# Differential attention in an fp32 hybrid block: where the memory's query linears stand in its pipeline, and where lambda is formed

## The chip, the cores and the metric

The kernel runs on one core of a Trainium2 chip. The metric is the device time of one execution in microseconds, and the median of several runs is compared.

## The reference, cut to what matters

Two blocks run one after the other; the change touches the second, a stack of two layers (`l` = 0, 1) over 512 tokens with 1024 features. Each layer forms many projections of the same input, among them the queries, keys and values of a differential attention and the queries of an attention over 256 memory vectors:

```python
lam = exp(sum(lf[0] * lf[1])) - exp(sum(lf[2] * lf[3])) + lam_init      # one number a layer
s = einsum('bqhcd,bkhcd->bhcqk', qi, k)        # 4 heads, two score maps c = 0, 1, 64 features each
p = softmax(s, axis=-1)
a = p[:, :, 0] - lam * p[:, :, 1]              # the two maps mixed
o = einsum('bhqk,bhkv->bqhv', a, v)
...
mx_q = x @ w_in[..., the last 512 columns]     # the memory's queries: the "query linears"
mx_o = memory_attention(mx_q, mem_k, mem_v)    # softmax over 256 memory vectors, 4 heads
```

## The kernel before, in words

Every engine has its own instruction list, written out by hand; an engine runs its list strictly in order and waits on semaphores. The order of the lists is therefore the schedule.

**Weights.** A linear in fp32 is done as three matmuls on split operands. Weights arrive in a ring of six slots (SyncE issues the loads). ScalarE rounds a slot's weights to the high part (`cast_to`, L402, tile WH), GpSimd subtracts to get the low part (`rest_to`, L411, tile WL), and TensorE uses both. WH and WL hold three pieces. `cast_to(act, n)` makes all casts up to piece n that are not made yet, where it stands in ScalarE's list.

**Token linears** (`tok_pe`, `tok_a`, `tok_v`, `tok_g`). Three groups of four pieces give the queries, keys and values. ScalarE empties their banks (L2329). VectorE rotates queries and keys (helper, L1765 to L1772), TensorE turns them per head (L2321), VectorE copies the turned queries (L2351) and ScalarE the turned keys (L2334). Lambda: a product and a sum on VectorE (L2358, L2360), Exp on ScalarE (L2337), two small operations on VectorE (L2362, L2364).

**The differential attention** (`diff`) runs over 16 items (4 heads by 4 blocks of 128 queries) as a pipeline of five stages over t = 0 to 19. At step t TensorE does, in this order, the values product of item t-4 (L2393), the turn of the mixed probabilities of item t-3 (L2386) and the scores of item t (L2379). ScalarE does the output copy of item t-4 (L2437), the copy of the turned probabilities of item t-3 (L2432) and the two Exps of item t-1 (L2425). VectorE does the two maxima of item t-1 (L2402, then L2404) and the mixing of item t-2 (L2407 to L2413).

**Beside it**, after the stages of every fourth step (`if t % 4 == 0`), one piece of other work is put in: on TensorE one of the memory's query linears (24 matmuls, L459 to L462), on ScalarE `cast_to` of the piece two further on and then the copy that empties that linear's bank (L2495). In layer 0 the first such place holds the memory's values instead (TensorE L2466, ScalarE L2478), and the four query linears follow; layer 1 begins with a query linear. Then comes `memory`, the attention over the memory, whose first scores are L2196; on VectorE the normalisation of the differential attention (L2537, L2539) stands ahead of its first maximum (L2202).

Banks are taken in turn from eight (`bank.take`), and a bank is taken again only after the copy that empties it.

Of the kernel before, what the change touches and what calls it, by code (L numbers as in the profile page):

```python
# [9 lines left out]
ALU = mybir.AluOpType  # L10
ACT = mybir.ActivationFunctionType
AX = mybir.AxisListType.X
# [32 lines left out]
ROWS = {"mla_q_norm": 0, "mla_k_norm": 96, "da_norm_g_2": 192, "hg_norm_g_2": 448, "da_lambda_2": 704}  # L45
# [231 lines left out]
def program(nc, dr, out):  # L277
    ctx = ExitStack()
    with ctx:
# [2042 lines left out]
                    m.then_inc(*da.pe.up("turn", l, h, x))  # L2322

        def tok_a(act, l):
            for g in L_tok[l].groups:
                cast_to(act, g.last + 2)
                for t in range(4):
                    act.wait_ge(*split.pe.at("used", g.last))
                    act.copy((qt, kt_, vt)[g.key][:, t, :], ps(L_tok[l].name, g.key, t)[:, :]).then_inc(  # L2329
                        *bank.emptied((L_tok[l].name, g.key, t), da.a, "tok", l, g.key, t))  # L2330
            cast_to(act, g.last + 3)
            for h in range(4):
                act.wait_ge(*da.pe.at("turn", l, h, 1))
                act.copy(kT2[:, h, :], ps("qk", l, h, 1)[:, :]).then_inc(  # L2334
                    *bank.emptied(("qk", l, h, 1), da.a, "turned", l, h))
            act.wait_ge(*da.v.at("lam sums", l))
            act.activation(sm[:, 76:78], sm[:, 76:78], ACT.Exp).then_inc(*da.a.up("lam", l))  # L2337

        def tok_v(dve, l):
            dve.wait_ge(*da.a.at("tok", l, 1, 3))  # L2340
            cos = sm[:, 96:128].rearrange("p (a b) -> p a b", a=4).unsqueeze(2).to_broadcast([128, 4, 8, 8])
            sin = sm[:, 128:160].rearrange("p (a b) -> p a b", a=4).unsqueeze(2).to_broadcast([128, 4, 8, 8])
            s1 = scr2[:, 0:256].rearrange("p (a b c) -> p a b c", a=4, b=8)
            s2 = scr2[:, 256:512].rearrange("p (a b c) -> p a b c", a=4, b=8)
            for x_ in (qt, kt_):
                x4 = x_.rearrange("p t (h c) -> p t h c", h=8)
                rotate_v(dve, da, x4[:, :, :, 0:8], x4[:, :, :, 8:16], cos, sin, s1, s2)
            da.v.mark("rotated", l)
            for h in range(4):
                dve.wait_ge(*da.pe.at("turn", l, h, 0))  # L2350
                dve.tensor_copy(qT2[:, h, :], ps("qk", l, h, 0)[:, :]).then_inc(  # L2351
                    *bank.emptied(("qk", l, h, 0), da.v, "turned", l, h))
            lam_init = 0.8 - 0.6 * math.exp(-0.3 * l)
            lr = rows[:, ROWS["da_lambda_2"] + 256 * l:ROWS["da_lambda_2"] + 256 * l + 256] \
                .rearrange("p (a b c) -> p a b c", a=2, b=2)
            lp = scr2[:, 0:128].rearrange("p (a c) -> p a c", a=2)
            dve.wait_ge(*da.v.now())
            dve.tensor_tensor(lp, lr[:, :, 0, :], lr[:, :, 1, :], ALU.mult).then_inc(*da.v.up())  # L2358
            dve.wait_ge(*da.v.now())
            dve.tensor_reduce(sm[:, 76:78], lp, AX, ALU.add).then_inc(*da.v.up("lam sums", l))  # L2360
            dve.wait_ge(*da.a.at("lam", l))
            dve.tensor_tensor(sm[:, 78:79], sm[:, 77:78], sm[:, 76:77], ALU.subtract).then_inc(*da.v.up())  # L2362
            dve.wait_ge(*da.v.now())
            dve.tensor_scalar(sm[:, 78:79], sm[:, 78:79], -lam_init, None, ALU.add).then_inc(*da.v.up("lam", l))  # L2364
# [115 lines left out]
        def mem_pe(pe, l, ready):  # L2480
            if l == 0:
                mem_values_pe(pe, l)
                yield
            for g in L_mq[l].groups:
                linear_pe(pe, L_mq[l], lambda g: [(hx, S, ready)], groups=[g])
                yield
# [9 lines left out]
                    *bank.emptied((L_mq[l].name, g.key, 0), mem.a, "mq", l, g.key))  # L2496
                yield

        def diff(run, beside, stages=(4, 3, 2, 1, 0)):


            for t in range(20):
                for stage in stages:
                    if 0 <= t - stage < 16:
                        run(stage, t - stage)
                if t % 4 == 0:
                    next(beside, None)
            last_of(beside)

# [517 lines left out]
        def tensor(pe):  # L3027
            pe.wait_ge(*lds["ident"])
            pe.wait_ge(*st0.g.at("ones"))
            side = adaln_pe(pe, range(0, 4))  # L3030
            next(side)
            next(side)
            for s, name in enumerate(("n0x", "n0c")):
                first_sums_pe(pe, name, (S, SC)[s], s)
            next(side)
            ring.ask(2)
            last_of(side)
            ring.ask(SPLITS)
            ring.here("inputs")
            in_pe(pe, filter_pe(pe))  # L3040
            side = adaln_pe(pe, (*range(4, 10), *range(12, 16)))
            mixer_pe(pe, side)
            out_pe(pe)
            sts = mod_streams("n1", 0, 3, "norm2")
            ffn_pe(pe, L_ffn0, lambda s: parts_done("n1", sts, s), spread(adaln_pe(pe, BESIDE[0])))
            totals_pe(pe, ["n2x", "n2c"])
            some_pe(pe, 16, 1)
            low_rank_pe(pe)
            latent_pe(pe)
            mla_out_pe(pe)  # L3050
            ring.here("mem0")
            sts = mod_streams("n3", 1, 3, "norm2")[0:1]
            ffn_pe(pe, L_ffn1, lambda s: parts_done("n3", sts, s), spread(adaln_pe(pe, BESIDE[1])))
            ln_pe(pe, ln_in, lin.v.at("res", L_ffn1.name, L_ffn1.groups[-1].key, 0))
            mem_keys_pe(pe, 0, lambda: whole_pe(pe, ln_in.name, S, 0))
            for l in range(2):
                ready = parts_done(ins_of[l].name, [ins_of[l]], 0, True)
                tok_pe(pe, l, ready)
                diff(lambda stage, i: da_pe(pe, l, stage, i), mem_pe(pe, l, ready))
                A = mem_attention(l)  # L3060
                memory(lambda stage, i: (scores_pe, Nothing(), turn_pe, values_pe)[stage](pe, A, i), iter(()))
                recur_in_pe(pe, l, ready)
                hv = hv_pe(pe, l, ready)
                recurrence(lambda at: [next(hv) for _ in range(HV_TILES[at])], lambda h: equal_pe(pe, l, h), lambda lev, h: level_pe(pe, l, lev, h),
                           lambda h: far_pe(pe, l, h), lambda h: recur_out_pe(pe, l, h), lambda h: iter(()),
                           lambda k: mix_turn_pe(pe, l, k))
                mix_pe(pe, l)
                ln_pe(pe, ln_1[l], lin.v.at("res", L_mix[l].name, 7, 0))
                if l == 0:
                    mem_keys_pe(pe, 1, lambda: whole_pe(pe, ln_1[0].name, S, 0))  # L3070
                else:
                    whole_pe(pe, ln_1[1].name, S, 0)
                ready1 = parts_done(ln_1[l].name, [ln_1[l]], 0, True)
                ffn_pe(pe, L_ffb[l], lambda s: ready1)
                ln_pe(pe, ln_2[l], lin.v.at("res", L_ffb[l].name, L_ffb[l].groups[-1].key, 0))
                if l == 0:
                    mem_values_pe(pe, 1, lambda: whole_pe(pe, ln_2[0].name, S, 0))
            whole_pe(pe, ln_2[1].name, S, 0)
# [3 lines left out]
        def vector(dve):  # L3082
# [30 lines left out]
            ln_v(dve, ln_in)  # L3113
            for l in range(2):
                tok_v(dve, l)
                diff(lambda stage, i: da_v(dve, l, stage, i), iter(()), (1, 2))
                A = mem_attention(l)
                memory(lambda stage, i: (Nothing(), exp_v, turn_v, values_v)[stage](dve, A, i), da_norm_v(dve, l),
                       (1, 3))
                recur_in_v(dve, l)  # L3120
                none_ = Nothing()
                recurrence(lambda at: hv_v(dve, l, at), lambda h: keys_v(dve, l, 0, h), lambda lev, h: level_v(dve, l, lev, h), lambda h: gain_v(dve, l, h), none_,
                           lambda h: finish_v(dve, l, h), lambda k: mix_low_v(dve, l, k))
                mix_v(dve, l, ins_of[l].name)
                ln_v(dve, ln_1[l])
                ffb_v(dve, l, ln_1[l].name)
                if l == 0:
                    ln_v(dve, ln_2[l])
# [10 lines left out]
        def scalar(act):  # L3139
# [34 lines left out]
            ln_a(act, ln_in, lambda: mem_keys_a(act, 0))  # L3174
            for l in range(2):
                tok_a(act, l)
                diff(lambda stage, i: da_a(act, l, stage, i), mem_a(act, l))
                A = mem_attention(l)
                memory(lambda stage, i: (Nothing(), exp_a, turn_a, Nothing())[stage](act, A, i), iter(()))
                cast_to(act, L_mq[l].groups[-1].last + 3)  # L3180
# [252 lines left out]
```

## Time and profile before

| | |
|---|---|
| median of 3 runs | 3419.32 us (3416.54 to 3421.88) |
| profiled execution | 3414.53 us, span 3412.7 us |
| TensorE busy | 3249.1 us, 95% of the span |
| VectorE, ScalarE, GpSimd busy | 1417.9, 1307.2, 1396.6 us |
| differential attention, layer 0 | 1857.41 to 1938.26 us |
| differential attention, layer 1 | 2678.44 to 2746.91 us |

The stretches of the two attentions run from the first scores to the first scores of the memory attention behind them; together they are 149 us, 4.4% of the span. Each row of the timeline below gives the start, the duration of the row's instructions together and, in brackets, the idle time of the engine before it with what ended it.

### The profile page before, as it was taken

The page shows a single profiled execution, that of the slowest core. Times are in us where ns is not written, and L with a number is a line of the kernel's source. Part 1 is how long each engine was busy: PE and PEld are TensorE (multiplying, and loading weights), DVE is VectorE, ACT ScalarE, POOL GpSimd, SP SyncE. Part 2 cuts the span into 40 slices and gives each one's busy share as a digit, 9 for nine tenths or more (in the row PEclk, how much of TensorE's full clock was granted, in tenths as well). Part 3 has the DMA queues.
Part 4 walks back from the last instruction along what each step waited for, and adds up shares of the span by engine and source line. Part 5 has one row for each costly group of instructions (what it writes and reads, how often), then busy time and mean ns, then how long its engine had stood idle before and what let it go on. Part 6 is the DMA issues. An engine that isn't in the chain of part 4 may idle for free.

```text
span 3412.7 us, 40302 instructions
## 1 busy us (share of the span) xinstructions
PE 3249.1 (95%) x16296; PEld 2573.9 (75%) x16296; DVE 1417.9 (42%) x2560; ACT 1307.2 (38%) x2309; POOL 1396.6 (41%) x788
## 2 busy tenths in 40 slices
PE   7989999999998889999999999999999989999998
PEld 4864788888874546788887688888887768878887
DVE  5566342222245664321222767243232658434132
ACT  4222332222244666432333534343333543444243
POOL 2224432222242433544463036544455215554445
PEclk9999999999998999999999999999999999999999
DMA  6135223121222000423233021322323112122322
GB/s 229 62 131 192 86 80 130 55 70 50 63 80 77 18 13 2 147 86 106 86 118 99 19 79 29 104 99 86 108 83 119 56 44 61 43 90 90 104 88 71
DMA packets 85639, 286.09 MB, mean 84 GB/s; under 512 B 9772, under 2 KB 10348, under 8 KB 84941
## 3 DMA queue, kind: packets, MB, share of 16 engines
q1 hardware_dynamic: 85452, 283.50, 25.6%
q8 instruction: 129, 2.11, 0.3%
q14 instruction: 58, 0.47, 0.0%
HBM read 281.37 MB, written 2.10 MB: 83 GB/s over the span
## 4 chain that ended last, share of the span: by engine, by line
PE 86%; DVE 8%; ACT 4%; DMA 1%; issue 1%; POOL 1%; SPq 0%; DVEq 0%; ACTq 0%
PE ps L459 20%; PE ps L462 20%; PE ps L460 20%; PE ps L1984 2%; PE ps L499 2%; PE ps L501 2%; PE ps L500 2%; DMA ring<-in_w_mod 1%; PE ps L2054 1%; PE ps L529 1%; PE ps L437 1%; PE ps L2028 1%; PE ps L438 1%; PE ps L2379 1%; PE ps L439 1%
## 5 line engine op out<-in xcount | busy, mean ns | idle before, releaser
L411 POOL TENSOR_TENSOR WL<-ring,WH 128x1024 fp32r<-128x1024 f32 (+2 forms) x443 | 962.3, 2176 | 1518.5 <-ACT WH L402 1518.2
L459 PE MATMUL ps<-HX,WH 128*128 128x512 f32 x1768 | 694.9, 393 | 3.1 <-POOL WL L411 3.1
L462 PE MATMUL ps<-HX,WL 128*128 128x512 f32 x1768 | 691.9, 391 | 0.0
L460 PE MATMUL ps<-HX,WH 128*128 128x512 f32 x1768 | 690.4, 390 | 0.0
L402 ACT CAST WH<-ring 128x1024 fp32r<-128x1024 f32 (+2 forms) x443 | 420.1, 950 | 371.0 <-PE ps L462 312.9
L459 PE MATMUL ps<-FR,WH 128*128 128x512 f32 x1120 | 418.9, 374 | 0.3
L460 PE MATMUL ps<-FR,WH 128*128 128x512 f32 x1120 | 409.5, 373 | 0.0
L459 PEld LDWEIGHTS ps<-HX,WH 128*128 128x128 f32 x1768 | 332.4, 188 | 82.9 <-issue 7.4
L462 PE MATMUL ps<-FR,WL 128*128 128x512 f32 x1120 | 389.2, 373 | 0.0
L462 PEld LDWEIGHTS ps<-HX,WL 128*128 128x128 f32 x1768 | 333.7, 189 | 49.8
L460 PEld LDWEIGHTS ps<-HX,WH 128*128 128x128 f32 x1768 | 332.5, 188 | 49.0
L910 DVE SCALAR_TENSOR_TENSOR T<-ps,pv,T 128x511 f32<-128x511 f32 (+1 forms) x154 | 109.4, 710 | 495.0 <-ACT T L906 494.9
L459 PEld LDWEIGHTS ps<-FR,WH 128*128 128x128 f32 x1120 | 210.2, 188 | 46.8 <-DVE FR L2969 1.1
L460 PEld LDWEIGHTS ps<-FR,WH 128*128 128x128 f32 x1120 | 210.3, 188 | 37.3
L906 ACT ACTIVATE T<-ps,pv 128x512 f32<-128x512 f32 (+1 forms) x154 | 113.1, 749 | 299.6 <-PE ps L462 290.9
L462 PEld LDWEIGHTS ps<-FR,WL 128*128 128x128 f32 x1120 | 198.5, 188 | 30.1
L867 DVE SCALAR_TENSOR_TENSOR X<-ps,mod,X 128x512 f32<-128x512 f32 x64 | 47.9, 750 | 340.2 <-PE ps L462 322.6
L1555 ACT CAST FR<-T 128x512 fp32r<-128x512 f32 x110 | 61.3, 576 | 254.9 <-DVE T L1583 152.4
L460 PE MATMUL ps<-HC,WH 128*128 128x256 f32 x504 | 141.6, 281 | 0.0
L462 PE MATMUL ps<-HC,WL 128*128 128x256 f32 x504 | 141.4, 280 | 0.0
L459 PE MATMUL ps<-HC,WH 128*128 128x256 f32 x504 | 141.3, 280 | 0.0
L499 PE MATMUL ps<-WH,HX 128*128 128x512 f32 x320 | 126.8, 396 | 0.8 <-ACT AR L2473 0.8
(390 smaller groups left out, 5074.8 us busy)
## 6 DMA issues: line engine op xcount, KB each, us to landing
ring<-in_w_mod SPq DMA_DIRECT2D x96, 512.0 KB, 5.5
ring<-in_ffn_w_up SPq DMA_DIRECT2D x88, 512.0 KB, 3.4
ring<-in_w_up SPq DMA_DIRECT2D x88, 512.0 KB, 3.4
ring<-in_w_in_tok SPq DMA_DIRECT2D x40, 512.0 KB, 3.5
ring<-in_w_in_feat SPq DMA_DIRECT2D x32, 512.0 KB, 3.4
ring<-in_ffn_w_down SPq DMA_DIRECT2D x32, 384.0 KB, 3.1
ring<-in_w_out SPq DMA_DIRECT2D x32, 384.0 KB, 3.1
ring<-in_w_down SPq DMA_DIRECT2D x32, 384.0 KB, 3.1
```

What stands on the lines that cost most here:

```text
L402: act.copy(WH[:, p % SPLITS, 0:n], ring.ap(r)).then_inc(*split.a.up("high", p))
L411: pool.tensor_tensor(WL[:, p % SPLITS, 0:n], ring.ap(r), WH[:, p % SPLITS, 0:n], ALU.subtract).then_inc(*ring.frees(r, split.g, "low", p))
L459: pe.matmul(o, high, xh, first, False)
L460: pe.matmul(o, high, xl, False, False)
L462: m = pe.matmul(PS[bs[i]][:, 0:N], low, get(k)[0], False, last)
L499: pe.matmul(PS[bs[t]][:, :], xh[:, tt], high, k == 0, False)
L500: pe.matmul(PS[bs[t]][:, :], xh[:, tt], low, False, False)
L501: m = pe.matmul(PS[bs[t]][:, :], xl[:, tt], high, False, k == 7)
L906: act.activation(dst, src, ACT.Identity, scale=w1, bias=b).then_inc(*steps.up("conv", *name))
L910: dve.scalar_tensor_tensor(dst[:, 1:N], src[:, 0:N - 1], w0, dst[:, 1:N], ALU.mult, ALU.add).then_inc(*steps.up())
L1555: act.copy(hidden(L, n, s)[0], d).then_inc(*fw.a.up("high", L.name, n, s))
L1984: pe.matmul(PS[b][:, 0:c1 - c0], QT[n % 2][0:96, h, t * 128:t * 128 + 128], KT[n % 2][0:96, h, c0:c1], True, True).then_inc(*att.pe.up("sc ...
```

## The change

Three edits. In `diff`, TensorE's piece beside the pipeline now follows the stages of steps 1, 5, 9, 13 and 17 and ScalarE's the stages of steps 2, 6, 10, 14 and 18 (both were 0, 4, 8, 12, 16). In `tok_a` and `tok_v`, lambda's product, sum and Exp are made ahead of the token linears' work. In `tok_a`, the cast of the third memory query piece (`cast_to(act, g.last + 3)`) follows the copies of the turned keys.

```diff
         def tok_a(act, l):
+            act.wait_ge(*da.v.at("lam sums", l))
+            act.activation(sm[:, 76:78], sm[:, 76:78], ACT.Exp).then_inc(*da.a.up("lam", l))
             for g in L_tok[l].groups:
...
-            cast_to(act, g.last + 3)
             for h in range(4):
                 act.wait_ge(*da.pe.at("turn", l, h, 1))
                 act.copy(kT2[:, h, :], ps("qk", l, h, 1)[:, :]).then_inc(
                     *bank.emptied(("qk", l, h, 1), da.a, "turned", l, h))
-            act.wait_ge(*da.v.at("lam sums", l))
-            act.activation(sm[:, 76:78], sm[:, 76:78], ACT.Exp).then_inc(*da.a.up("lam", l))
+            cast_to(act, g.last + 3)
...
-        def diff(run, beside, stages=(4, 3, 2, 1, 0)):
+        def diff(run, beside, at, stages=(4, 3, 2, 1, 0)):
...
-                if t % 4 == 0:
+                if t % 4 == at:
                     next(beside, None)
...
-                diff(lambda stage, i: da_pe(pe, l, stage, i), mem_pe(pe, l, ready))
+                diff(lambda stage, i: da_pe(pe, l, stage, i), mem_pe(pe, l, ready), 1)
...
-                diff(lambda stage, i: da_a(act, l, stage, i), mem_a(act, l))
+                diff(lambda stage, i: da_a(act, l, stage, i), mem_a(act, l), 2)
```

In `tok_v` the product and the sum (L2353 to L2360) stand at the head of the function; the two small operations after the Exp stay where they were. VectorE has nothing beside the pipeline, so its place there has no effect.

## Rows read from the trace of the kernel before

**Rows 1.** The page: busy time of the engines (share of the span), instructions

```profile
PE 3249.1 (95%) x16296; PEld 2573.9 (75%) x16296; DVE 1417.9 (42%) x2560; ACT 1307.2 (38%) x2309; POOL 1396.6 (41%) x788
```

**Rows 2.** Timeline, ends of the turns and first scores, layer 1 (start, us, engine, line)

```profile
2673.20 3.65 PE L2321 MATMUL ps<-ident,AR 128*128 128x128 f32 x32
2675.31 1.08 ACT L402 CAST WH<-ring 128x1024 fp32r<-128x1024 f32 x1
2676.26 2.09 ACT L2334 COPY AR<-ps 128x512 f32<-128x512 f32 x4
2678.44 1.13 PE L2379 MATMUL ps<-AR 64*128 64x512 f32 x4 [1.59 <-ACT AR L2334]
```

**Rows 3.** Timeline of TensorE, the fill in layer 0, then layer 1's second linear

```profile
1872.40 1.99 PE L2379 MATMUL ps<-AR 64*128 64x512 f32 x8
...
1876.65 0.63 PE L2386 MATMUL ps<-ident,AR 128*128 128x128 f32 x4 [2.26 <-ACT AR L2425]
1881.05 0.50 PE L459 MATMUL ps<-HX,WH 128*128 128x512 f32 x1
...
2693.81 0.50 PE L459 MATMUL ps<-HX,WH 128*128 128x512 f32 x1
```

**Rows 4.** Timeline of TensorE, one query linear and the items behind it, layer 0

```profile
1896.86 0.50 PE L459 MATMUL ps<-HX,WH 128*128 128x512 f32 x1
...
1902.45 1.05 PE L2393 MATMUL ps<-AR 128*128 128x128 f32 x8
1903.34 0.60 PE L2386 MATMUL ps<-ident,AR 128*128 128x128 f32 x4
1903.87 1.13 PE L2379 MATMUL ps<-AR 64*128 64x512 f32 x4
1904.93 1.16 PE L2393 MATMUL ps<-AR 128*128 128x128 f32 x8
...
1912.68 0.50 PE L459 MATMUL ps<-HX,WH 128*128 128x512 f32 x1
```

**Rows 5.** Timeline of ScalarE in the same stretch

```profile
1897.10 0.68 ACT L2425 ACTIVATE AR<-ps,sm 128x512 f32<-128x512 f32 x1
1897.76 1.04 ACT L402 CAST WH<-ring 128x1024 fp32r<-128x1024 f32 x1
...
1905.14 0.69 ACT L2425 ACTIVATE AR<-ps,sm 128x512 f32<-128x512 f32 x1
1906.13 0.27 ACT L2437 COPY AR<-ps 128x128 f32<-128x128 f32 x1 [0.21 <-PE ps L2393]
```

**Rows 6.** Timeline of GpSimd and VectorE in the same stretch

```profile
1898.88 2.40 POOL L411 TENSOR_TENSOR WL<-ring,WH 128x1024 fp32r<-128x1024 f32 x1 [41.09 <-ACT WH L402]
1899.06 2.24 DVE L2404 TENSOR_SCALAR sm<-sm 128x2 f32<-128x2 f32 x1
1905.03 1.29 DVE L2402 TENSOR_REDUCE sm<-ps 128x1 f32<-128x512 f32 x2 [2.28 <-PE ps L2379]
1906.70 0.48 DVE L2411 TENSOR_SCALAR AR<-AR,sm 128x512 f32<-128x512 f32 x1
1907.21 0.75 DVE L2413 SCALAR_TENSOR_TENSOR AR<-AR,sm 128x512 f32<-128x512 f32 x1
1907.88 1.28 DVE L2402 TENSOR_REDUCE sm<-ps 128x1 f32<-128x512 f32 x2
```

**Rows 7.** Timeline of GpSimd and VectorE where the rotation of layer 1 meets it

```profile
2654.51 0.42 DVE L1768 TENSOR_TENSOR AR<-AR,sm 128x256 f32<-128x256 f32 x1
2654.70 2.49 POOL L411 TENSOR_TENSOR WL<-ring,WH 128x1024 fp32r<-128x1024 f32 x1 [4.93 <-ACT WH L402]
2654.85 2.62 DVE L1769 TENSOR_TENSOR AR<-AR,sm 128x256 f32<-128x256 f32 x1
```

**Rows 8.** Timeline, the end of the pipeline in layer 0

```profile
1938.76 0.69 DVE L2537 TENSOR_TENSOR AR<-AR 128x512 f32<-128x512 f32 x1 [7.66 <-ACT AR L2437]
```

**Rows 9.** TensorE's granted clock behind it (us, TensorE busy, clock, DMA share, GB/s)

```profile
1945.00:1955.00 10.00, 7.58 (x35) 0.83 0.01 2
```

More of the change, by code:

```diff
@@ L2335, in tok_a @@
                     *bank.emptied(("qk", l, h, 1), da.a, "turned", l, h))
-            act.wait_ge(*da.v.at("lam sums", l))
-            act.activation(sm[:, 76:78], sm[:, 76:78], ACT.Exp).then_inc(*da.a.up("lam", l))
+            cast_to(act, g.last + 3)
         def tok_v(dve, l):
+            lam_init = 0.8 - 0.6 * math.exp(-0.3 * l)
+            lr = rows[:, ROWS["da_lambda_2"] + 256 * l:ROWS["da_lambda_2"] + 256 * l + 256] \
+                .rearrange("p (a b c) -> p a b c", a=2, b=2)
+            lp = scr2[:, 0:128].rearrange("p (a c) -> p a c", a=2)
+            dve.wait_ge(*da.v.now())
+            dve.tensor_tensor(lp, lr[:, :, 0, :], lr[:, :, 1, :], ALU.mult).then_inc(*da.v.up())
+            dve.wait_ge(*da.v.now())
+            dve.tensor_reduce(sm[:, 76:78], lp, AX, ALU.add).then_inc(*da.v.up("lam sums", l))
             dve.wait_ge(*da.a.at("tok", l, 1, 3))
@@ L2352, in tok_v @@
                     *bank.emptied(("qk", l, h, 0), da.v, "turned", l, h))
[L2353 to L2360, printed above, removed]
             dve.wait_ge(*da.a.at("lam", l))
@@ L3115, in vector @@
                 tok_v(dve, l)
-                diff(lambda stage, i: da_v(dve, l, stage, i), iter(()), (1, 2))
+                diff(lambda stage, i: da_v(dve, l, stage, i), iter(()), 0, (1, 2))
                 A = mem_attention(l)
```

## The prediction

> **What bounds the kernel.** I read the page first. TensorE is busy 95% of the span [rows 1], so a change gains where TensorE stands idle and loses where it is made to wait. Then I read the timeline of the two stretches that are touched, engine by engine, because a share says nothing about which wait ends last. The reader should see three things.
>
> First, an ordinary step of the pipeline costs TensorE 2.59 us: values 1.00, turn 0.53, scores 1.06. The step right behind a linear is 2.48 (1902.45 to 1904.93), and a linear is 5.59 (1896.86 to 1902.45) [rows 4]. From the values behind one linear to the next linear are 10.23 us, which is 2.48 and three times 2.59 [rows 4]: TensorE waits for nothing there.
>
> Second, VectorE needs more for an item than TensorE does. Its maxima start at 1905.03 and again at 1907.88, 2.85 us later [rows 6]. It falls 0.26 us back per step and catches up while TensorE is in a linear.
>
> Third, the linear also hides ScalarE's cast (1897.76), which comes 0.66 after the second Exp (1897.10) [rows 5], and GpSimd's pass that follows it 1.12 later and lasts 2.40 (1898.88). That pass stops VectorE: a scaling of two columns, L2404, lasts 2.24 us and ends as the pass does [rows 6]. TensorE is in the linear and doesn't notice.
>
> TensorE's real waits lie at the fill: 2.26 us ahead of the first turn in layer 0 [rows 3], and 1.59 ahead of the first scores [rows 2].
>
> **Part 1: the cast behind the key copies.** ScalarE makes the cast at 2675.31 and only then the four key copies, which end at 2678.35; the scores follow at 2678.44. TensorE's turns end at 2673.20 + 3.65 = 2676.85 [rows 2]. Without the cast the last key copy starts at about 2676.90, takes 0.59 and ends at 2677.49. The scores start at 2677.58, which is 0.86 us earlier. Both layers show the same pattern, so 1.7 us in all. The cast piece is read three linears later; its slot in SyncE's queue comes free some 2 us later, and the load in it (the first hgrn piece) is needed tens of microseconds on. Nothing waits.
>
> **Part 2: lambda.** The product, the sum and the Exp with its table load leave the stretch ahead of the pipeline. There they were already covered: by the memory values in layer 0 and by the first linear in layer 1. At the new place ScalarE has them ahead of the cast of a layer's fourth token piece. The three pieces before it are cast already, and each holds TensorE 24 matmuls, about 5.4 us as a query linear does, so some 5 us can be lost there unseen. VectorE is done with its norm by then. Cost and gain: nothing. If the cover were gone, the cost would lie between nothing and, from the nearest row, three Exps of 0.69 (2.1 us) a layer.
>
> **Part 3: the linears one step on, at the fill.** In layer 0 TensorE goes from 1872.40 to 1881.05, so 8.65 us, between the memory values and the first linear [rows 3]. Its work there is two scores, turn, scores, values, turn, scores: 4 x 1.06 + 2 x 0.53 + 1.00 = 6.30. So 2.35 are waits, since ScalarE stood blocked behind the memory values. After the change the scores of item 1 come first and Exp 0 and mixing 0 run under the values. The values take 13.93 (they start 1.06 after the 1857.41 of the table and end at 1872.40), so they end at 1856.55 + 2 x 1.06 + 13.93 = 1872.60. Then: scores 2, turn 0 (ready), scores 3, values 0, 3.65 us. Turn 1 needs mixing 1: VectorE starts maximum 2 1.16 after scores 2 (1903.87 to 1905.03) and ends mixing 1 about 3.05 later (a maximum and a mixing, 2.85, plus the signal), at 4.21, so 0.56 of wait. Turn 2 waits 0.26 by VectorE's longer period. The linear starts 8.65 after 1872.60, at 1881.25, with one item more done than before (2.59): gain 2.39. By the same sum layer 1, with a linear in place of the values, starts its second linear at 2693.94 (2693.81 before [rows 3]) with an item more: 2.46. Parts 1 and 3 together gain 4.85 us.
>
> **Part 4: the banks emptied a further step on.** This is where I expect the loss. ScalarE reaches the cast and the copy in step 4k+2, behind that step's output copy, and that waits for values that TensorE makes only after the linear. So both land in the open, between the second Exp and the next output copy. Let D be the start of the values behind the linear (1902.45, [rows 4]). The second Exp is at D + 2.69, the cast at D + 3.35; it holds ScalarE 0.95 (2675.31 to 2676.26). The bank's copy holds it about 0.49, as a key copy does (four in 2.09, [rows 2]). The output copy starts at D + 4.79 (now D + 3.68, 1906.13, [rows 5]), their turned copy at D + 5.05 and is ready at D + 5.69 (0.59 and the signal), and TensorE wants them at D + 5.07: 0.62 us of wait. Queued behind are the next Exps, which stay in time.
>
> GpSimd's pass now starts at D + 3.35 + 1.12 = D + 4.47. VectorE is then in L2411 (D + 4.25 to D + 4.73), and L2413 is due at D + 4.76 [rows 6]. Who gets in? Layer 1's rotation shows the same meeting: GpSimd comes at 2654.70 during L1768, gets in when that ends, and L1769, due at 2654.85, takes 2.62 instead of 0.42 [rows 7]. So L2413 ends some 0.5 after the pass, near D + 7.64, its signal at D + 7.79. The turn that needs it is due at D + 6.69 after the 0.62: another 1.10. The next turn adds 0.26. Sum: 1.98 us for each linear with a cast in the open. These are three whole blocks (layer 0 step 10; layer 1 steps 6 and 10): 5.9 us. Linears without a cast (the first of each layer, whose pieces are cast already) cost nothing: 0.49 fits in.
>
> The Trainium skill, page "SBUF — State Buffer", section "SBUF: two separate sides", says that VectorE and GpSimd share one pair of ports, that whoever starts first holds it for its whole instruction, and that a VectorE instruction with two SBUF inputs needs it. L2413 has two. By this rule L2413 would wait as L1769 does, and the sum would be the same; the rule also says that had L2413 started first, GpSimd would wait instead, which would make a block cost about 0.9 and not 1.98.
>
> **Last blocks.** The last block of layer 1 (cast at step 14) has no linear behind it, and the same two waits fall in it: 1.98, less 0.05 since the drain at the end gives a little back: 1.9. In layer 0 the cast at step 14 costs 1.98 again. Its last linear now stands between steps 17 and 18, not 16 and 17. One wait of a values product for its turned copy is then inside the linear, but another takes its place at step 17, and turn 14 comes 0.3 to 0.6 later as VectorE is behind: 2.4 for the block. In layer 0 the cast of step 18 then puts GpSimd's pass at about 1940.3 to 1942.7, onto L2537, which now runs free at 1938.76 [rows 8] and would be due at 1940.9: 1.6 more, as the memory attention's maxima stand behind it.
>
> **Sum.** -4.85 + 5.9 + 1.9 + 2.4 + 1.6 = +7.0 us. Against the profiled execution's own 3414.53 that is 3421.5. Its time is 4.8 below the median, so against the median I forecast 3426.3. A change under 0.2%, 6.8 us, can hardly be told from none here; my forecast lies on that edge.
>
> **Rivals.**
> - *GpSimd's pass costs nothing*: it meets only VectorE's reads of PSUM, as L2402. Then only 0.62 a block remain, and the gains outweigh them: -2 us, 3417.3. For it: L2402 is not slowed. Against: 4.47 lies 0.2 inside L2411, and a shift of 0.2 either way is needed. Chance 0.10.
> - *The other side, faster*: ScalarE takes the cast and copy in its own idle time, and the whole 4.85 stays: 3414.5. It decides at 1.44 us of slack a step; the rows show ScalarE idle about 0.4 in a step (0.21 of it at 1906.13). Chance 0.07.
> - *Worse by the clock*: behind layer 0's attention the granted clock is 0.83 in 1945 to 1955 [rows 9], so TensorE ran some 3.4 us at 1.2 GHz after waits. Longer waits there lengthen this. If it takes 5 us more, half of that is lost: +2.5, 3428.8; in both layers 3431. Chance 0.15.
> - The forecast's mechanism, with its price between +4 (layer 0's end absorbed) and +9: 0.68.
>
> **Numbers.** The likeliest is 3426.3; its own range is 3422 to 3429. The range that leaves two in ten out reaches to the first rival's 3417.3 and to one clock loss and the spread of medians: 3417 to 3430. Slower by over 0.2% (above 3426.2): half of the 0.68 and nearly all of the 0.15, 0.46. Faster by over 0.2% would need 6.8 us of gain where the whole gain found is 4.85: 0.03. Within: 0.51.
>
> **What would show it.** In the trace after: first scores 0.86 earlier; no wait of 2 us ahead of the first turn; the first linear of layer 0 at about 1881.3 and 12.2 us (now 10.23) from the values behind the second linear to the third; L2413 at some 2.9 us in three or four places, overlapping L411; a wait of TensorE at L2386 just after; L2537 late in layer 0. If blocks keep 10.2 us, step 4 is wrong and the kernel is faster. If L2413 is not stretched but L2393 waits 0.6, the first rival holds.

## The result and the profile after

The changed kernel takes 3428.41 us, the median of 7 runs (3421.27 to 3434.62); the kernel before takes 3418.94 in 7 runs beside it (3414.24 to 3421.88). The ratio is 1.0027 with a 95% interval of 1.0017 to 1.0036: slower by 9.5 us, by 5.8 at least. The forecast was 3426.3. A second comparison (r1_changed, below) gave 1.0029 [1.0017, 1.0040], with 3429.60 against 3421.36.

The profiled execution took 3429.68 us, its span is 3427.9. The page's busy row answers to [rows 1]:

```profile
PE 3268.8 (95%) x16296; PEld 2584.2 (75%) x16296; DVE 1417.5 (41%) x2560; ACT 1305.9 (38%) x2309; POOL 1393.7 (41%) x788
```

The counts of instructions are the same and only their order changed. The share is 95% again, so this row can't say where the time went. A TensorE that runs at a lower clock counts as busier too: e2_head_only, below, has a row of eight products that lasts 2.08 us instead of 1.16.

**The head and the fill, layer 0.** The timeline of the changed kernel answers to [rows 2] and [rows 3] (start, us, engine, line; in brackets the idle time before it and what ended it):

```profile
1857.61 3.65 PE L2321 MATMUL ps<-ident,AR 128*128 128x128 f32 x32
1861.78 1.05 ACT L402 CAST WH<-ring 128x1024 fp32r<-128x1024 f32 x1
1861.98 1.99 PE L2379 MATMUL ps<-AR 64*128 64x512 f32 x8 [0.72 <-ACT AR L2335]
1863.90 14.00 PE L2466 MATMUL ps<-ring,CX 128*128 128x512 f32 x32
1877.83 1.13 PE L2379 MATMUL ps<-AR 64*128 64x512 f32 x4
1878.89 0.66 PE L2386 MATMUL ps<-ident,AR 128*128 128x128 f32 x4
...
1880.54 1.16 PE L2393 MATMUL ps<-AR 128*128 128x128 f32 x8
1882.07 0.63 PE L2386 MATMUL ps<-ident,AR 128*128 128x128 f32 x4 [0.38 <-DVE AR L2413]
...
1886.47 0.50 PE L459 MATMUL ps<-HX,WH 128*128 128x512 f32 x1
```

The wait ahead of the first scores is 0.72 us and not 1.59, since the cast now stands behind the key copies. The wait of 2.26 ahead of the first turn is gone; a smaller one, 0.38 for a mixing, stands three instructions on. The first linear starts 28.86 us after the turns (1857.61 to 1886.47), where it started at 28.89 before, and one item more is done by then.

**One block with a cast in the open, layer 0.** This answers to [rows 4 to 6]. The rows are picked out of the timelines of four engines; PEld is TensorE's loading of weights:

```profile
1907.88 1.05 PE L2393 MATMUL ps<-AR 128*128 128x128 f32 x8
1911.22 1.05 ACT L402 CAST WH<-ring 128x1024 fp32r<-128x1024 f32 x1
1911.88 2.06 PE L2379 MATMUL ps<-AR 64*128 64x512 f32 x4
1912.12 0.48 DVE L2411 TENSOR_SCALAR AR<-AR,sm 128x512 f32<-128x512 f32 x1
1912.16 0.60 ACT L2495 COPY AR<-ps 128x512 f32<-128x512 f32 x1
1912.35 2.46 POOL L411 TENSOR_TENSOR WL<-ring,WH 128x1024 fp32r<-128x1024 f32 x1 [47.10 <-ACT WH L402]
1912.63 0.29 ACT L2437 COPY AR<-ps 128x128 f32<-128x128 f32 x1
1912.64 2.73 DVE L2413 SCALAR_TENSOR_TENSOR AR<-AR,sm 128x512 f32<-128x512 f32 x1
1912.79 0.62 ACT L2432 COPY AR<-ps 128x512 f32<-128x512 f32 x1
1912.81 0.29 PEld L2379 LDWEIGHTS ps<-AR 64*128 64x128 f32 x2 [0.64 <-ACT AR L2495]
1913.86 1.16 PE L2393 MATMUL ps<-AR 128*128 128x128 f32 x8
...
1915.42 0.66 PE L2386 MATMUL ps<-ident,AR 128*128 128x128 f32 x4 [0.39 <-DVE AR L2413]
...
1919.90 0.50 PE L459 MATMUL ps<-HX,WH 128*128 128x512 f32 x1
```

The values behind the linear start at 1907.88; call it D as the prediction did. The cast starts at D + 3.34 (forecast 3.35), GpSimd's pass at D + 4.47 (4.47), and L2413 at D + 4.76 (4.76). L2413 needs 2.73 us where it needed 0.75 [rows 6]. From the values to the next linear are 12.02 us, where 10.23 stood [rows 4]. The bracket on TensorE shows only 0.39 of waiting: most of the wait is hidden in rows that last longer. The four scores at 1911.88 take 2.06 instead of 1.13. A row counts from its first instruction to its last, so a wait inside it is no idle time ahead of it. It is safer to read the distance from one landmark to the next.

What the scores wait for stands in the rows of the weight loads. Four of them belong to the two score maps of an item, two to each. In the kernel before they go out together:

```profile
1903.87 0.30 PEld L2379 LDWEIGHTS ps<-AR 64*128 64x128 f32 x4 [0.17 <-ACT AR L2437]
```

In the changed kernel the two of the second map start at 1912.81, 0.93 us behind the first map's (1911.88), and what ended their wait is L2495, the copy that empties the query linear's bank. A step of the pipeline takes four banks and a linear one, so of the eight banks the linear's own comes round again at the second map of the second step behind it. The two maps run side by side in 1.13 us; 0.93 apart, they take 2.06.

**The end of layer 0's pipeline** answers to [rows 8]. Timeline, and behind it the windows of TensorE's granted clock (us, busy, clock, DMA share, GB/s):

```profile
1945.00 2.35 POOL L411 TENSOR_TENSOR WL<-ring,WH 128x1024 fp32r<-128x1024 f32 x1 [12.57 <-ACT WH L402]
1945.46 1.13 PE L2196 MATMUL ps<-AR 128*128 128x256 f32 x4 [0.27 <-ACT AR L2495]
1945.61 2.29 DVE L2538 TENSOR_TENSOR AR<-AR 128x512 f32<-128x512 f32 x1 [8.17 <-ACT AR L2437]
1948.54 0.41 DVE L2202 TENSOR_REDUCE sm<-ps 128x1 f32<-128x256 f32 x1
...
1945.46:1953.46 8.00, 4.80 (x17) 0.69 0.20 66
1953.46:1961.46 8.00, 5.87 (x32) 0.89 0.01 2
```

L2538, the line that was L2537 before, lasts 2.29 us and not 0.69. The first maxima of the memory attention (L2202) follow 3.08 us behind its first scores (1945.46 to 1948.54), where they followed by 1.83 before.

**The two stretches by landmarks.** All executions are compared from here on by the distance, in us, from the start of the head turns (L2321) to the four linears, to the first scores of the memory attention and to its first maxima. Each figure is the difference of two starts in the timeline.

| | linears, layer 0 | scores, maxima | linears, layer 1 | scores, maxima |
|---|---|---|---|---|
| before | 28.89, 44.70, 60.52, 75.12 | 86.10, 87.93 | 6.30, 20.61, 36.44, 52.26 | 73.71, 75.54 |
| changed | 28.86, 44.67, 62.29, 78.68 | 87.85, 90.93 | 6.29, 20.63, 38.26, 55.87 | 76.44, 78.27 |

Linear to linear is 15.82 before and 17.62 after wherever a cast stands in the open. The maxima come 3.00 us later in layer 0 and 2.73 later in layer 1, 5.73 together.

### The profile page after: what moved, and what is told of

It reads as the page before. It is cut to its first block, busy times and chain, and to the rows that moved or that the text cites. A ratio compares the mean times of both kernels' runs of the same rounds, so it can differ in the third digit from the quotient of the medians.

```text
span 3427.9 us, 40303 instructions
## 1 busy us (share of the span) xinstructions
PE 3268.8 (95%) x16296; PEld 2584.2 (75%) x16296; DVE 1417.5 (41%) x2560; ACT 1305.9 (38%) x2309; POOL 1393.7 (41%) x788
## 4 chain that ended last, share of the span: by engine, by line
PE 86%; DVE 8%; ACT 4%; DMA 1%; issue 1%; POOL 1%; SPq 0%; DVEq 0%; ACTq 0%
PE ps L459 20%; PE ps L462 20%; PE ps L460 20%; PE ps L1984 2%; PE ps L499 2%; PE ps L500 2%; PE ps L501 2%; DMA ring<-in_w_mod 1%; PE ps L529 1%; PE ps L2054 1%; PE ps L1226 1%; PE ps L437 1%; PE ps L2028 1%; PE ps L438 1%; PE ps L439 1%
## 5 line engine op out<-in xcount | busy, mean ns | idle before, releaser
L499 PE MATMUL ps<-WH,HX 128*128 128x512 f32 x320 | 126.8, 396 | 0.8 <-ACT AR L2473 0.8
```

What stands on the lines that cost most here:

```text
L499: pe.matmul(PS[bs[t]][:, :], xh[:, tt], high, k == 0, False)
```

## The experiments

Three mechanisms were to be told apart: ScalarE's cast and copy in the open; GpSimd's pass stopping VectorE; and the clock. Times are compared with runs of the kernel before on the same chip. The sum of a kernel is the maxima's distance in both layers together: 163.47 before, 169.20 changed.

**e1_same_step: ScalarE's casts and copies in the linear's own step.** The linears stay one step on, and the casts lie under them again.

```diff
-                diff(lambda stage, i: da_a(act, l, stage, i), mem_a(act, l), 2)
+                diff(lambda stage, i: da_a(act, l, stage, i), mem_a(act, l), 1)
```

> ScalarE's cast and bank copy stand in the same step as the linear (1, 5, 9, ...), everything else as in the changed kernel. Stretch = start of the turns to the first scores of the memory attention (before 86.10 and 73.71 us, changed kernel 87.85 and 76.44). Theory (the loss comes from emptying a further step on: cast, copy and GpSimd's pass in the open): the casts lie under the linears again, 15.8 us from one linear to the next, L2413 0.75 us everywhere; stretches about 84.0 and 71.1, so 4.8 us faster than before in all, 0.14%. Rival (the loss comes from the linears standing an item on): linears stay 17.6 apart and the stretches stay at 87 and 76. Rival (the pass costs nothing, only copies do): stretches between, 85 and 72.

Measured: 3413.96 us in 5 runs (3407.50 to 3415.38) against 3421.77, ratio 0.9967 [0.9954, 0.9979]. Timeline of ScalarE, GpSimd and VectorE at one linear, and VectorE at the end of the pipeline:

```profile
1901.14 1.04 ACT L402 CAST WH<-ring 128x1024 fp32r<-128x1024 f32 x1
1902.26 2.40 POOL L411 TENSOR_TENSOR WL<-ring,WH 128x1024 fp32r<-128x1024 f32 x1 [39.06 <-ACT WH L402]
1902.44 2.24 DVE L2404 TENSOR_SCALAR sm<-sm 128x2 f32<-128x2 f32 x1
...
1939.71 0.69 DVE L2538 TENSOR_TENSOR AR<-AR 128x512 f32<-128x512 f32 x1 [7.86 <-ACT AR L2437]
```

The pass stops VectorE just as long as before, on L2404 as in [rows 6], and costs nothing, because TensorE is in its linear. The blocks are 15.81 us again (28.87, 44.68, 60.50) and the sum is 158.20: 5.27 less than before, 11.00 less than the changed kernel. So the whole loss hangs on ScalarE's place, and the gain at the head and fill is real.

**r2_same_step**, the same kernel again, on another occasion and with more runs.

> The version with cast and bank copy in the linear's own step once more. Theory: 3 to 8 us faster than before by the stretches' 5.3 us. Rival (the 11 us measured first are the effect): 9 or more again.

Measured: 3414.04 us in 11 runs against 3421.36, ratio 0.9979 [0.9971, 0.9988]; sum 158.19.

**e2_head_only: the places of before, with lambda and the first cast as in the change.**

```diff
-                diff(..., mem_pe(pe, l, ready), 1)
+                diff(..., mem_pe(pe, l, ready), 0)
-                diff(..., mem_a(act, l), 2)
+                diff(..., mem_a(act, l), 0)
```

> Both places beside the pipeline back at steps 0, 4, ...; lambda ahead and the cast behind the key copies stay. Theory: first scores 0.88 us earlier in each layer, the fill's wait of over 2 us ahead of the first turn stays or grows a little, stretches about 85.3 and 72.9: 1.7 us faster than before in all (0.05%, not to be told in the time). Rival (lambda's early Exp holds back the first token casts): turns start later against the end of the norm and the total is the same or slower.

Measured: 3423.64 us in 11 runs, ratio 1.0002 [0.9992, 1.0013]. In layer 0 all landmarks come 0.88 earlier than before (28.01 for the first linear, 87.05 for the maxima): the cast's move gives what was forecast. Layer 1 does not show it: its second linear starts at 21.05, 0.44 *later* than before, where 0.87 earlier was due: 1.3 us are lost. The windows of TensorE there, and a row of its timeline inside:

```profile
2683.00:2687.00 4.00, 2.18 (x10) 1.00 0.00 2
2687.00:2691.00 4.00, 3.66 (x17) 0.73 0.00 0
2691.00:2695.00 4.00, 4.00 (x17) 0.85 0.00 0
...
2689.11 2.08 PE L2393 MATMUL ps<-AR 128*128 128x128 f32 x8
```

TensorE was busy 2.18 of 4 us while it waited for its first turn; behind that the granted clock is 0.73 of full, a part of the window at the lower of its two levels (1.2 GHz), and eight values products take 2.08 us, where they take 1.16 at 2.4 GHz. No theory had this, and it led to the last runs.

**e3_pass_held: GpSimd's pass waits for a later mixing.** All is as in the changed kernel, but the pass of a cast in the open is held until VectorE has done the mixing that L2413 ends.

```diff
-                for g in L_mq[l].groups:
+                for g, i in zip(L_mq[l].groups, (0, 11, 15, 15) if l == 0 else (0, 7, 11, 15)):
+                    if i:
+                        pool.wait_ge(*da.v.at("mixed", l, i))
```

> As the changed kernel, but GpSimd's pass waits for a later mixing, so that it starts when TensorE is in the next linear (in each layer's last place it waits for the last mixing). Casts and bank copies stay where the change put them. Theory (two terms, ScalarE's 0.62 to 0.9 and VectorE's 1.1 to 1.2 of a port held by GpSimd): L2413 is 0.75 us again, and from linear to linear it is 16.5 to 16.8 us instead of 17.6 (15.8 before). Stretches about 86 and 74. Rival (GpSimd's pass costs nothing; ScalarE alone sets the wait): still 17.6. Rival (the pass is all of it): 15.8.

Measured: 3422.64 us in 11 runs, ratio 0.9993 [0.9984, 1.0002]; sum 164.25. Timeline of one block:

```profile
1916.46 1.05 ACT L402 CAST WH<-ring 128x1024 fp32r<-128x1024 f32 x1
1917.12 2.05 PE L2379 MATMUL ps<-AR 64*128 64x512 f32 x4
1917.39 0.60 ACT L2495 COPY AR<-ps 128x512 f32<-128x512 f32 x1
1917.88 0.75 DVE L2413 SCALAR_TENSOR_TENSOR AR<-AR,sm 128x512 f32<-128x512 f32 x1
1918.05 0.29 PEld L2379 LDWEIGHTS ps<-AR 64*128 64x128 f32 x2 [0.64 <-ACT AR L2495]
...
1924.80 2.40 POOL L411 TENSOR_TENSOR WL<-ring,WH 128x1024 fp32r<-128x1024 f32 x1 [54.31 <-DVE AR L2413]
```

L2413 is at its 0.75 again, and the block takes 16.74 us (44.67 to 61.42; 16.73 in layer 1). So of the 1.80 that a block loses, the pass adds 0.88 to the 0.92 that is left with ScalarE. The scores still last 2.05: the second map starts at 1918.05, again 0.93 behind the first, and waits for the bank that L2495 empties. That copy stands behind the cast.

**e4_split: the cast in the linear's step, the bank's copy alone one step on.**

```diff
             if l == 0:
+                yield
                 mem_values_a(act, l)
                 yield
             for g in L_mq[l].groups:
                 cast_to(act, g.last + 2)
+                yield
                 act.wait_ge(*split.pe.at("used", g.last))
...
-                if t % 4 == at:
+                if t % 4 in at:
...
-                diff(..., mem_pe(pe, l, ready), 1)
+                diff(..., mem_pe(pe, l, ready), (1,))
-                diff(..., mem_a(act, l), 2)
+                diff(..., mem_a(act, l), (1, 2))
```

> As the changed kernel, but ScalarE's cast stands in the linear's own step and only the bank's copy a step further on. Theory: cast and GpSimd's pass are under the linear again and a copy of 0.59 us alone fits into ScalarE's step (the first linears, which have no cast, showed no loss): 15.8 from linear to linear, stretches about 84 and 71, as with both in the same step. Rival (the bank's late emptying is what costs, through the scores that take that bank next): 16.3 or more from linear to linear.

Measured: 3415.11 us in 11 runs, ratio 0.9979 [0.9970, 0.9988]; sum 158.19. The landmarks are those of e1_same_step to 0.02 us. The copy in the open costs nothing. The changed kernel's loss in a block comes with the cast's loss of cover: the cast holds back the bank's copy, and sets off the pass.

**e6_cast_late: the reverse, the copy in the linear's step, the cast one step on.**

`at` is as in e4_split.

```diff
                 mem_values_a(act, l)
                 yield
+                yield
             for g in L_mq[l].groups:
-                cast_to(act, g.last + 2)
                 act.wait_ge(*split.pe.at("used", g.last))
...
                 yield
+                cast_to(act, g.last + 2)
+                yield
```

> As the changed kernel, but ScalarE's bank copy stands in the linear's own step and only the cast, with GpSimd's pass behind it, a step further on. Theory (VectorE's held port is the larger term and ScalarE's work alone the smaller): L2413 is 2.7 us again in the steps behind the casts and the linears are 17.0 to 17.7 us apart, although ScalarE has 0.49 us less in the open. Rival (ScalarE's load is what counts, the port only follows): about 16.4.

One run: 3430.65 us. The blocks with a cast in the open take 17.63 us in layer 0 and 17.61 in layer 1: as long as in the changed kernel, though no copy stands behind the cast. The timeline of layer 1's last whole block, whose values (L2393) start at 2724.80, and the clock behind it:

```profile
2728.15 1.05 ACT L402 CAST WH<-ring 128x1024 fp32r<-128x1024 f32 x1
2729.28 2.46 POOL L411 TENSOR_TENSOR WL<-ring,WH 128x1024 fp32r<-128x1024 f32 x1 [15.14 <-ACT WH L402]
2729.57 2.72 DVE L2413 SCALAR_TENSOR_TENSOR AR<-AR,sm 128x512 f32<-128x512 f32 x1
...
2732.35 0.66 PE L2386 MATMUL ps<-ident,AR 128*128 128x128 f32 x4 [1.28 <-DVE AR L2413]
...
2740.00:2750.00 10.00, 8.72 (x53) 1.00 0.00 0
2750.00:2760.00 10.00, 7.88 (x36) 0.58 0.18 54
```

The two waits are not a sum. With the copy behind the cast TensorE loses 0.92 by ScalarE and what is left of the pass behind that. With the copy gone, the values ahead of the turn start only 0.04 late (at 5.11 us behind 2724.80, where 5.07 is due), and the pass takes the rest of the 1.80, 1.28 of it in one bracket. The turn starts 7.55 us behind the block's first values; in the changed kernel it was 7.54. What ends last is L2413, whatever ScalarE does. At the end of this run the clock also fell to 0.58, and the sum is 173.08: 3.9 more than in the changed kernel, 2.8 of it in the last block of layer 1, where that fall lies, and 1.1 in the last block of layer 0.

**e5_lambda_only: lambda at its new place, all the rest as before.** It is e2_head_only with `cast_to(act, g.last + 3)` back ahead of the key copies.

> Of the change only lambda's product, sum and Exp ahead of the token linears; the cast and both places beside the pipeline as before. Theory (covered at both places): stretches 86.10 and 73.71 us to 0.1, first scores 5.25 behind the turns. Rival (the early Exp holds back the token casts): a gap of TensorE in the token linears, ahead of the turns. Rival (it frees the pipeline's start): first scores earlier.

One run: 3423.37 us. Layer 1 is as before to 0.03 us (6.30, 20.64; 75.57). The token linears take as long as before: from their first matmul (L499) to the turns are 66.61 us in layer 0 and 65.72 in layer 1, in the kernel before 66.63 and 65.72. One wait of TensorE of 0.8 us stands near their start in layer 0, in both kernels alike. ScalarE has the table load, the Exp and the cast behind it while TensorE has work left. The rows of the changed kernel:

```profile
1799.91 1.28 ACT L2326 ACT_TABLE_LOAD   x1
1801.21 0.20 ACT L2326 ACTIVATE sm<-sm 128x2 f32<-128x2 f32 x1
1801.32 1.03 ACT L402 CAST WH<-ring 128x1024 fp32r<-128x1024 f32 x1
```

Layer 0's fill, though, took 1.36 us more than before (30.25 instead of 28.89), at a clock of 0.80 and 0.77 in 1882 to 1890. That is e2_head_only's effect again, in the other layer. Either lambda's move brings it, or the kernel before has it too, in some executions.

**b1_before, b2_before, b3_before: the kernel before, profiled three more times.**

> The kernel before, profiled again, for its granted clock in the fill of the pipeline (layer 0: from the end of the memory values to the first linear, 8.65 us; layer 1: from the first to the second linear, 14.31 us). Lambda alone and head alone each showed one fill of two that was 1.3 to 1.4 us longer, with TensorE at 1.2 GHz in it. Theory (the fill's waits of 2.2 us let the clock fall in some executions, so the kernel before pays for them more than the first trace shows): some of the six fills of these three profiles are 1.3 us longer. Rival (it comes from lambda's new place): none is.

> As the run ahead of it: the kernel before, a second profile of the fills.

> As the run ahead of it: the kernel before, a third profile of the fills.

Times 3418.69, 3420.51 and 3423.42 us. The kernel before has it too. The windows of TensorE over layer 0's fill in b2_before:

```profile
1874.00:1878.00 4.00, 1.85 (x8) 1.00 0.39 131
1878.00:1882.00 4.00, 3.88 (x14) 0.58 0.00 0
1882.00:1886.00 4.00, 4.00 (x21) 0.99 0.03 8
```

and the same stretch in b3_before:

```profile
1881.00:1885.00 4.00, 2.21 (x9) 1.00 0.36 131
1885.00:1889.00 4.00, 3.52 (x22) 1.00 0.00 0
```

The wait is the same and the clock is not. Where the clock fell, the fill took 1.3 to 1.4 us more: in layer 1 of b1_before, in both layers of b2_before, in none of b3_before or of the profile that the prediction read. That is 3 fills of 8, and with e2_head_only and e5_lambda_only, which keep the same wait, 5 of 12. It happened in none of the 14 fills of the seven profiles in which the linears stand one step on. The sums of the kernel before are 163.47, 164.85, 166.31 and 163.48, so 164.5 on average. The profile that the prediction was made against was one of the lucky ones.

The Trainium skill, page "TensorE: Matmul & The Clock Gate", section "Part 1: The HAM clock gate", says of the start of a kernel that the number of its slow matmuls varies from run to run. No run here shows that for the start. For a fall of the clock inside the kernel these four profiles of one kernel do vary, with 0, 1, 2 and 0 fills at the lower clock.

**r1_changed: the changed kernel again.**

> The changed kernel itself once more, on the chip of the other runs of this call. The stretches are expected again at 87.85 and 76.44 us (to the memory attention's first scores), 5.7 us more than before to its first maxima. Theory (all of the change's cost is in the two stretches, the rest of the first measurement's 9.5 us is scatter): the total is 4 to 9 us above before. Rival (there is a second cost outside the stretches, of some 4 us): again 9 or more, and between the stretches and behind them the same places are longer in this profile as in the first.

Measured: 3429.60 us in 7 runs (3424.29 to 3435.54) against 3421.36, ratio 1.0029 [1.0017, 1.0040]; the landmarks are those of the first profile (90.93 and 78.30, sum 169.23), with a span of 3422.5.

## Why the forecast held, point by point

The forecast, 3426.3, lies 2.1 us below the measured 3428.41. That it lies so close is in part luck: the terms were 1.3 us too high for the two stretches (7.0 against 5.73), and 3.7 of the measured 9.5 lie outside them, where the forecast had nothing. Its chances leaned to no measurable change (0.51) over slower (0.46); the measured 0.27% is slower. Its terms against the two profiles, by the landmarks:

| term | forecast | measured |
|---|---|---|
| cast behind the key copies, and fill, layer 0 | -2.39 | -2.62 (an item of 2.59 more, 0.03 earlier) |
| the same, layer 1 | -2.46 | -2.57 |
| both | -4.85 | -5.19 |
| three blocks with a cast in the open | +5.9 | +5.39 (1.80, 1.80, 1.79) |
| last block, layer 1 | +1.9 | +1.71 |
| last block, layer 0 | +2.4 | +2.57 |
| L2537 under GpSimd's pass | +1.6 | +1.25 |
| lambda | 0 | 0 |
| sum | +7.0 | +5.73 |

**Part 1** gave 0.88 in layer 0 where 0.86 was forecast, and e2_head_only shows it alone. **Part 2** is free: e5_lambda_only. **Part 3** was right in its order of events and in its waits: from the end of the memory values (1877.83) to the linear are 8.64 us, where 8.65 was forecast, and from values 0 to turn 1 (1880.54 to 1882.07) are 1.53, so 0.53 of wait where 0.56 was forecast; the bracket shows only 0.38 of it. The gain is 0.34 larger over both layers mainly because two score groups in a row take 1.92 us (1861.98 to 1863.90) and not twice 1.06.

**Part 4** was right in the pass and in what it stops, and its place was met to 0.01 us. The term for a block, 0.62 by ScalarE, 1.10 by the pass and 0.26 behind it, came to 1.80 instead of 1.98. Three things in it were off. ScalarE's part alone is 0.92 (e3_pass_held), not 0.62: the working followed the output copies and forgot that the second score map waits for the bank that L2495 empties. The values behind it start at D + 5.98 (1913.86), where the working had them at 5.69. The parts were taken as a chain in which each adds its wait, but the turn waits for L2413 alone, so a ScalarE part of 0.92 or of 0.04 (e6_cast_late) gives the same block, and taking the copy away saves nothing. And the end of L2413 was put too late: D + 7.64, though the working's own terms (4.47, 2.40 and some 0.5) give 7.37; it ended at D + 7.49 (1912.64 + 2.73). The turn follows at D + 7.54 and not 7.79, and behind it 0.31 is lost and not 0.26 (4.48 us to the linear, 4.17 before).

By the Trainium skill, page "SBUF — State Buffer", section "SBUF: two separate sides", a VectorE instruction with two SBUF inputs waits for as long as GpSimd's instruction holds the shared ports; the trace agrees, with 2.73 us against 0.75 for L2413. **The rival in which the pass costs nothing** falls with it: its forecast of 0.62 a block is below even the 0.92 without the pass. **The faster side** falls too, as the fill's gain was there and the blocks took more. Its gain of 4.85 is nevertheless about what e1_same_step reaches by the landmarks (5.27), with the casts under the linears.

**The clock rival** is partly seen. In the 32 us behind the first memory scores of layer 0 the clock is 0.69, 0.89, 1.00, 1.00 in four windows of 8 us, against 1.00, 0.79, 0.99, 1.00 before: 3.4 us of full clock lost against 1.8. But the work from the maxima of layer 0 to the turns of layer 1 took 734.37 and 733.32 us in the two profiles of the changed kernel, and 733.11 to 734.65 in the four of the kernel before. So its price isn't shown.

**What was not foreseen** is that the baseline itself varies, by the fill's clock. It makes the stretches of the kernel before 164.5 on average and not 163.47, which leaves 4.7 us of loss in them for the changed kernel.

**What stays open.** The medians differ by 9.5 and 8.2 us; the stretches give 4.7 to 5.7. The interval begins at 5.8. The mean span of the two profiles of the changed kernel is 7.7 us above that of the four of the kernel before (3425.2 and 3417.5). Of this the stretches hold 4.7, the part ahead of layer 0's turns 1.5, and the rest 1.6. The part ahead, in which only lambda for layer 0 stands at another place, varies between 1850.4 and 1862.9 us over all thirteen profiles, and between 1852.2 and 1861.0 in those of the kernel before alone. Lambda isn't the reason: the token linears that it stands in take 66.64 us in the changed kernel and 66.63 before. So 2.5 to 4.8 us of the medians' differences are not placed: chance in the choice of executions would do, and so would a clock that falls more often elsewhere. The runs of r1_changed lean to the clock. Their mean granted clock is 0.981 in seven, against 0.983 in the seventeen of the kernel before beside them, and 0.002 of the span is some 7 us of full clock. A part of that lies in the stretches themselves; where the rest falls, no run shows.

**The better version** is the one with the casts in the linear's own step. e1_same_step and r2_same_step are faster than the kernel before by 0.33% and 0.21%, e4_split by 0.21%, each with its interval wholly below 1. By the landmarks they gain 5.3 us against the first profile and 6.3 against the mean of four, since the wait of 2.2 us at the fill, on which the clock fell, is gone.

## What to carry to other kernels

A cast under a long linear was free here, and with it all that the cast set off on other engines; before an item is moved by a step, ask what covers it now and which engine it will start. Where two waits can hold the same product, find which ends last: removing the earlier one may save nothing. And a change of under 0.3% should be judged against more than one profile of the kernel before, because a wait of 2 us on TensorE may or may not bring its clock down.

## What the runs showed of the hardware

- The same wait of 2.2 us on TensorE was followed by a fall of the granted clock (0.57 to 0.69 in the 4 us from the wait's end) in 5 of 12 fills and by none in 7; where it fell, the fill cost 1.3 to 1.4 us more.
- Two products of 64 rows each, on different halves of the rows, run side by side: the two score maps take 1.13 us together (1903.87) and 2.06 when the second starts 0.93 later (1911.88).
- GpSimd's pass begins inside L2411 (1912.35, while L2411 runs from 1912.12 to 1912.60). L2411 keeps its 0.48 us, and L2413, due 0.04 later, is the one that pays. The rows don't show whether the pass has the ports from its start or from L2411's end; either way VectorE's next instruction comes too late to keep it out.
- A tiny instruction is stopped as long as a large one: L2404, with two columns, lasted 2.24 us under the pass and 0.17 without it; L2413, with 512, lasted 2.73 and 0.75.
